# Building the PEER gate matrix in two half-width pieces inside the expert loop, on eight cores

## The reference, cut to what matters

```python
scores = jnp.einsum("thpd,hpkd->thpk", qry, sub_keys)
s_top, i_top = lax.top_k(scores, PEER_TOPK)
cand = s_top[:, :, 0, :, None] + s_top[:, :, 1, None, :]
cand_idx = i_top[:, :, 0, :, None] * 128 + i_top[:, :, 1, None, :]
best, pos = lax.top_k(cand.reshape(n_tok, 8, -1), PEER_TOPK)
idx = jnp.take_along_axis(cand_idx..., pos, axis=-1)
gate = jax.nn.softmax(best, axis=-1)
...
act = gelu(einsum("td,thkd->thk", tb, u_tab[ib]))
out = einsum("thk,thkd->td", gb * act, v_tab[ib])
```

## Time and profile before

| what | us |
|---|---|
| median of 3 executions | 8333.69 (8250.29 to 8431.59) |
| the profiled execution's own time | 8357.25 |
| its slowest core (core 4), first to last instruction | 8355.7 |
| the other cores | 8289.5 to 8339.1 |
| start of the first scatter on core 4 | 4684.88 |

### The profile page before, as it was taken

The page is one execution under the profiler, slowest core; times in us unless marked ns, Lnnn a source line. Parts: engine busy times, 40 slices in busy tenths (PEclk is TensorE's granted clock), DMA queues, the critical chain, the costliest instruction groups (busy, mean ns, idle before and its releaser), DMA issues.

```text
span 8355.7 us, 116273 instructions; the slowest of 8 cores (8289.5 to 8355.7 us)
## 1 busy us (share of the span) xinstructions
PE 5202.0 (62%) x37168; PEld 3963.2 (47%) x37168; DVE 3898.4 (47%) x6582; ACT 2563.6 (31%) x4998; POOL 2637.1 (32%) x2252
## 2 busy tenths in 40 slices
PE   2666666666666666666662185675848485775949
PEld 2555555555555544554551153444535253543635
DVE  3343333344444444444433854547374654547260
ACT  1333333334343333334330122222222222222221
POOL 3222222222222222222210334334353534344353
PEclk7777777778888777777775587786968686777868
DMA  3133334330000000000002054363625254452637
GB/s 66 26 54 54 51 52 57 57 61 11 11 9 16 11 21 21 21 15 17 21 26 56 0 187 152 127 212 101 212 82 197 88 200 136 143 195 101 212 103 238
DMA packets 225330, 714.45 MB, mean 86 GB/s; under 512 B 20704, under 2 KB 70496, under 8 KB 220512
## 3 DMA queue, kind: packets, MB, share of 16 engines
q1 hardware_dynamic: 215520, 625.16, 22.6%
q0 software_dynamic: 9216, 81.86, 7.2%
HBM read 763.62 MB, written 92.27 MB: 102 GB/s over the span
## 4 chain that ended last, share of the span: by engine, by line
PE 42%; DVE 29%; issue 14%; ACT 9%; DMA 2%; POOL 2%; DVEq 1%; ACTq 0%; POOLq 0%; SPq 0%
PE p_bank L202 41%; DVE arena L236 18%; ACT arena L225 5%; ACT L225 3%; POOL arena L236 2%; PE p_bank L207 1%; DVE arena L261 1%; DVE arena L1096 1%; ACT arena L230 1%; DVE arena L1093 1%; DVE arena L247 1%; DVEq L166 1%; DVE arena L1092 1%; DVE arena L1095 1%; DMA arena<-w_in_tm 1%
## 5 line engine op out<-in xcount | busy, mean ns | idle before, releaser
L202 PE MATMUL p_bank<-arena 128*128 128x512 bf16 (+10 forms) x36160 | 5067.6, 305 | 2511.1 <-DVE arena L236 1099.8
L202 PEld LDWEIGHTS p_bank<-arena 128*128 128x128 bf16 (+3 forms) x36160 | 3844.4, 145 | 3720.7 <-issue 3147.5
L236 POOL TENSOR_TENSOR arena<-arena 128x256 bf16<-128x256 bf16 (+3 forms) x2128 | 2529.3, 1195 | 4798.2 <-ACT arena L225 1634.6
L236 DVE TENSOR_TENSOR arena<-arena 128x512 f32<-128x512 f32 (+8 forms) x1984 | 2394.9, 1232 | 1157.0 <-ACT arena L225 889.0
L225 ACT ACTIVATE arena<-p_bank 128x256 bf16<-128x256 f32 (+6 forms) x1648 | 632.7, 384 | 2008.8 <-PE p_bank L202 1921.9
L236 DVE TENSOR_TENSOR arena<-arena,p_bank 128x512 f32<-128x512 f32 (+2 forms) x688 | 420.5, 611 | 1633.5 <-PE p_bank L202 1541.9
L230 ACT COPY arena<-p_bank 128x512 f32<-128x512 f32 (+3 forms) x1120 | 607.3, 547 | 1128.9 <-PE p_bank L202 1010.8
L225 ACT ACT_TABLE_LOAD x341 | 437.5, 1283 | 995.8 <-DVE arena L236 723.9
L230 ACT CAST arena<-p_bank 128x512 bf16<-128x512 f32 x688 | 398.2, 581 | 952.7 <-PE p_bank L202 915.0
L207 PE MATMUL p_bank<-arena 128*128 128x128 f32 (+1 forms) x1008 | 164.1, 312 | 623.2 <-DVE arena L236 539.1
L207 PEld LDWEIGHTS p_bank<-arena 128*128 128x128 f32 (+1 forms) x1008 | 128.4, 157 | 651.9 <-issue 651.7
(11 more groups left out here) (30 smaller groups left out, 668.7 us busy)
## 6 DMA issues: line engine op xcount, KB each, us to landing
arena<-UT_bf SPq DMA_DIRECT2D x512, 512.0 KB, 5.5
arena<-V_bf SPq DMA_DIRECT2D x512, 512.0 KB, 4.4
UT_bf<-UT POOLq DMA_DIRECT2D x16, 2048.0 KB, 24.4
V_bf<-Vt POOLq DMA_DIRECT2D x16, 2048.0 KB, 35.7
arena<-xT SPq DMA_DIRECT2D x48, 528.0 KB, 5.0
arena<-x_scr SPq DMA_DIRECT2D x32, 512.0 KB, 4.7
ob_scr<-arena SPq DMA_DIRECT2D x16, 512.0 KB, 3.1
arena<-ob_scr SPq DMA_DIRECT2D x16, 512.0 KB, 5.9
```

The lines of the kernel that those rows point to most:

```text
L202: self.P.op("pe", lambda e: e.matmul(o, lhsT=l, rhs=r, start=start, stop=stop), reads=_bufs(lhsT, rhs), writes=_bufs(out))
L236: self.P.op(eng, lambda e: e.tensor_tensor(out=o, in0=x, in1=y, op=op), reads=_bufs(a, b), writes=_bufs(out))
```

## The change: what it does

The gate matrix becomes two tiles, `GsH[0]` for columns 0 to 63 and `GsH[1]` for columns 64 to 127. A half is made by 32 steps, each of which makes the full `Ac` (DVE comparison of 1024 elements and POOL product of 1024 elements, as before), half of `Bc` (512 elements), eight matmuls of 64 columns into one bank, the "prep" bank, and one copy of 512 elements, on ACT for even steps and on DVE for odd ones. So `Ac` is made twice for every block.

The steps are called in the expert loop. In its first half (i2 = 0 to 63) the 32 steps for this block's columns 64 to 127 are mixed with the 80 prep steps of the next block, two of these 112 steps after each iteration, until i2 = 55. In its second half the 32 steps for the next block's columns 0 to 63 follow, one after each of i2 = 64 to 95. Ahead of block 0 one half is made on its own. The last block has no prep and no second list; its 32 steps stand after i2 = 0 to 31.

```diff
-    Gs = P.sb("Gs", [128, TB, 128], BF16)
+    GsH = [P.sb("GsA", [128, TB, 64], BF16), P.sb("GsB", [128, TB, 64], BF16)]
...
-    def scatter(pb):
+    def scatter_half_steps(pb, hf):
         aT_ = abwT[pb]; a16_ = abT16[pb]
+        st = []
         for sb_i in range(TB // TS):
-            t0 = sb_i * TS
-            Ac = Acol[sb_i % 2]; Bc = Bcol[sb_i % 2]
-            io_bc = (iot16, iot16.t.unsqueeze(1).to_broadcast([128, TS, 128]))
-            O.tt(V(Ac), io_bc, (a16_, bc_last(a16_.t[:, 0, t0:t0 + TS], 128)), ALU.is_equal)
-            O.tt(V(Ac), V(Ac), (aT_, bc_last(aT_.t[:, 2, t0:t0 + TS], 128)), ALU.mult, eng="pool")
-            O.tt(V(Bc), io_bc, (a16_, bc_last(a16_.t[:, 1, t0:t0 + TS], 128)), ALU.is_equal)
-            for q4 in range(TS // 4):
-                bk = pbank("loop" if (sb_i * (TS // 4) + q4) % 4 else "prep")
-                for q in range(4):
-                    tl = q4 * 4 + q
-                    O.mm((bk, pv4(bk)[:, q, :]), (Ac, Ac.t[:, tl, :]), (Bc, Bc.t[:, tl, :]))
-                O.cp((Gs, Gs.t[:, t0 + q4 * 4:t0 + q4 * 4 + 4, :]), (bk, pv4(bk)), eng="act")
+            def s_sc(sb_i=sb_i):
+                t0 = sb_i * TS
+                ci = sc_ctr[0]; sc_ctr[0] += 1
+                Ac = Acol[ci % 2]; Bc = Bcol[ci % 2]
+                io_bc = (iot16, iot16.t.unsqueeze(1).to_broadcast([128, TS, 128]))
+                io_h = (iot16, iot16.t[:, 64 * hf:64 * hf + 64].unsqueeze(1).to_broadcast([128, TS, 64]))
+                O.tt(V(Ac), io_bc, (a16_, bc_last(a16_.t[:, 0, t0:t0 + TS], 128)), ALU.is_equal)
+                O.tt(V(Ac), V(Ac), (aT_, bc_last(aT_.t[:, 2, t0:t0 + TS], 128)), ALU.mult, eng="pool")
+                O.tt((Bc, Bc.t[:, :, 0:64]), io_h, (a16_, bc_last(a16_.t[:, 1, t0:t0 + TS], 64)), ALU.is_equal)
+                bk = pbank("prep")
+                for tl in range(TS):
+                    O.mm((bk, bk.t[:, tl * 64:(tl + 1) * 64]), (Ac, Ac.t[:, tl, :]), (Bc, Bc.t[:, tl, 0:64]))
+                O.cp((GsH[hf], GsH[hf].t[:, t0:t0 + TS, :]), (bk, bk.t[:, 0:TS * 64].rearrange("p (t i) -> p t i", t=TS)),
+                     eng=("act" if sb_i % 2 == 0 else "dve"))
+            st.append(s_sc)
+        return st
...
-    def expert_loop(pb, side):
+    def expert_loop(pb, side1, side2):
         hT_ = h2T[pb]
-        per = (len(side) + 127) // 128 if side else 0
+        side = side1
+        per = (len(side1) + 59) // 60 if side1 else 0
...
-                O.tt(V(ga), V(ab), (Gs, Gs.t[:, :, i2]), ALU.mult, eng="pool")
+                gh = GsH[i2 // 64]
+                O.tt(V(ga), V(ab), (gh, gh.t[:, :, i2 % 64]), ALU.mult, eng="pool")
...
                 for _ in range(per):
                     if si < len(side):
                         side[si](); si += 1
+                if i2 == 63:
+                    while si < len(side):
+                        side[si](); si += 1
+                    side = side2; si = 0
+                    per = (len(side2) + 59) // 60 if side2 else 0
...
     for blk in range(NB):
         pb = blk % 2
-        scatter(pb)
-        side = prep_steps(blk + 1, 1 - pb) if blk + 1 < NB else []
-        expert_loop(pb, side)
+        pr_ = prep_steps(blk + 1, 1 - pb) if blk + 1 < NB else []
+        sh_ = scatter_half_steps(pb, 1)
+        side1 = []
+        for i in range(max(len(pr_), len(sh_))):
+            if i < len(sh_):
+                side1.append(sh_[i])
+            lo = (i * len(pr_)) // max(1, len(sh_)); hi = ((i + 1) * len(pr_)) // max(1, len(sh_))
+            side1 += pr_[lo:hi] if i < len(sh_) else []
...
+        side2 = scatter_half_steps(1 - pb, 0) if blk + 1 < NB else []
+        expert_loop(pb, side1, side2)
         final(blk)
```

More of the change, by code:

```diff
@@ L1146, in prep_steps @@
         return st
-    def scatter(pb):
+    sc_ctr = [0]
+    def scatter_half_steps(pb, hf):
         aT_ = abwT[pb]; a16_ = abT16[pb]
+        st = []
         for sb_i in range(TB // TS):
-            t0 = sb_i * TS
-            Ac = Acol[sb_i % 2]; Bc = Bcol[sb_i % 2]
-            io_bc = (iot16, iot16.t.unsqueeze(1).to_broadcast([128, TS, 128]))
-            O.tt(V(Ac), io_bc, (a16_, bc_last(a16_.t[:, 0, t0:t0 + TS], 128)), ALU.is_equal)
-            O.tt(V(Ac), V(Ac), (aT_, bc_last(aT_.t[:, 2, t0:t0 + TS], 128)), ALU.mult, eng="pool")
-            O.tt(V(Bc), io_bc, (a16_, bc_last(a16_.t[:, 1, t0:t0 + TS], 128)), ALU.is_equal)
-            for q4 in range(TS // 4):
-                bk = pbank("loop" if (sb_i * (TS // 4) + q4) % 4 else "prep")
-                for q in range(4):
-                    tl = q4 * 4 + q
-                    O.mm((bk, pv4(bk)[:, q, :]), (Ac, Ac.t[:, tl, :]), (Bc, Bc.t[:, tl, :]))
-                O.cp((Gs, Gs.t[:, t0 + q4 * 4:t0 + q4 * 4 + 4, :]), (bk, pv4(bk)), eng="act")
+            def s_sc(sb_i=sb_i):
[14 more added lines that the diff above has]
+        return st
     NG = 128 // IG
@@ L1214, in final @@
                      (obank[tt][dh], obank[tt][dh].t[:, :]), ALU.add)
-            O.act((Gs, Gs.t[:, 0:8, :].rearrange("p a b -> p (a b)")), V(xb), AF.Square, accum=(smf, smf.t[:, tt:tt + 1]))
+            O.act((GsH[1], GsH[1].t[:, 0:16, :].rearrange("p a b -> p (a b)")), V(xb), AF.Square, accum=(smf, smf.t[:, tt:tt + 1]))
             O.act((smf, smf.t[:, tt:tt + 1]), (smf, smf.t[:, tt:tt + 1]), AF.Sqrt, scale=1.0 / 1024, bias=EPS)
@@ L1222, in phase2_build @@
         s_()
+    for s_ in scatter_half_steps(0, 0):
+        s_()
     for blk in range(NB):
         pb = blk % 2
-        scatter(pb)
-        side = prep_steps(blk + 1, 1 - pb) if blk + 1 < NB else []
-        expert_loop(pb, side)
+        pr_ = prep_steps(blk + 1, 1 - pb) if blk + 1 < NB else []
[6 more added lines that the diff above has]
+            side1 += pr_[lo:hi] if i < len(sh_) else []
+        if len(pr_) and len(sh_) == 0:
+            side1 = pr_
+        side2 = scatter_half_steps(1 - pb, 0) if blk + 1 < NB else []
+        expert_loop(pb, side1, side2)
         final(blk)
```

## The result

The changed kernel takes 9918.71 us (median of 10 executions, 9877.92 to 9942.69) where the kernel before, in the same session, takes 8314.54 (8234.48 to 8431.59): a ratio of 1.1964, with a 95% interval of 1.192 to 1.2008. It is 20% slower. The forecast of 9700 was 2.2% low and its range of 9150 to 10150 holds the result.

The account below looks back on a forecast made before the run. Before, DVE bound the scatter and PE the loop; mixed in, a ring of waits binds scatter iterations. 144 + 7 x 640 + 412 = 5036 us against 3671, +1365 on 8357, gives 9722, forecast as 9700; range 9150 to 10150.

Parts of the forecast that it names:

- The ring through PE, ACT, POOL and PE again: Scatter iterations: U, Gelu, GA, product and scatter matmuls wait in a circle, costing their sum, 6.3 us against 1.98 plain.
- The steps are hidden: Rival, chance 0.05: in the loop, scatter matmuls find their product finished; a gain of 612 us, time about 7720.
- it cancels: Rival, chance 0.05: a scatter iteration takes 4.0 us, which would give the time of the kernel before.
- slow throughout: Rival, chance 0.12: PE at 1.2 GHz and the product at 2.74 us; scatter iteration 7.4 us, time 10300.
- the ring alone, fast: Rival, chance 0.16: PE stays at 2.4 GHz and DVE keeps up; scatter iteration 5.2 us, time 8820.
- One sign of being wrong: First half of the loop: the prediction is wrong if PE's waits lie on DVE for much longer than 4 us.
- first half of the loop: Per block, 32 scatter and 80 prep steps over 56 iterations, then 8 plain: 2 x (48 + 122) + 16 = 356 us.
- Two tenths for the odd steps: Scatter iteration: DVE's copy and then its next comparison on odd steps raise 6.1 to 6.3 us.
- The product 2.1: POOL's product in a scatter iteration: 2.1 us, the mean of 1.8 alone and 2.4 behind a half comparison.
- I leave it: Final part of a block: kept at 19 us, since the next block's first scatter step waits on DVE behind the adds.
- DMA: nothing: Loads of the kernel: the same loads over a longer time, so no cost.
- DVE's 255 and POOL's 224 fit under: Loop, if the steps were hidden: DVE's 255 us and POOL's 224 us of work per block fit under its time.

Follow-up runs that it names:

- e1: The changed kernel with each scatter step's eight matmuls and copy called one scatter step later: 8825.84 us, ratio 1.070 to the kernel before.
- e3: The changed kernel with all scatter copies on ACT, none on DVE: 9427.74 us, ratio 1.1392 to the kernel before.
- e11: The changed kernel with both half scatters ahead of the loop, not mixed in, and prep steps one per iteration: 9500.21 us, ratio 1.139.
- e2: The changed kernel with the next block's first table loads issued before this block's final stores: 9954.33 us, ratio 1.206.
- e6: The changed kernel with matmuls and copy one scatter step later and all scatter copies on ACT: 8703.99 us, ratio 1.056.
- e12: The changed kernel with eight idle 512-column matmuls on PE ahead of each scatter step's matmuls in the loop: 9627.42 us, ratio 1.1549.

## Why the prediction was right, and where it was off

**The mechanism is shown.** The ring through PE, ACT, POOL and PE again was forecast from the order of the calls, and e1 removes most of it by that order alone. "The steps are hidden" and "it cancels" are out by the ratio; "slow throughout" by the windows (clock 0.63 and 0.75 in the two parts with scatter, products of 1.85 with DVE idle), "the ring alone, fast" by the same clock. One sign of being wrong was there in part: PE's waits for DVE in the first half, 78.6 us in 12 waits up to 8.9, are longer than the 4 us named. The forecast did count DVE's side in that half, and the half came out 14 us over.

**Direction and size of each term.** By the loop ends of core 5 (5495.3, 6159.7, 6822.8, 7487.0, 8152.3, 8820.8, 9482.8) a block is 664.6 us in the mean, where 640 was forecast. In the fourth block:

| term | forecast | measured |
|---|---|---|
| half ahead of block 0 | 144 | 138.4 |
| boundary | 19 | 23.5 |
| first half of the loop | 356 | 369.7 |
| 32 scatter iterations | 202 (6.3 each) | 212 (6.63 each) |
| 32 plain iterations | 63 | 59 |
| last block | 412 | 409.4 |

Seven blocks are 172 us over, and phase 2 begins at 4711.6 on this core where it began at 4684.9 on core 4 before. Together 199; less 6 for the half ahead and 3 for the last block, it makes the 190 by which the span of 9912 exceeds 9722. Phase 1 is untouched, and I take those 27 us as spread between cores and executions: in the kernel before, POOL's first product starts between 4674 and 4791 on its eight cores.

**Where a step of it was off.**

- *"Two tenths for the odd steps".* e3 shows 0.9, and a ring of 5.75, not 6.1, without them: two errors that all but cancelled, and that is luck. What I had missed is the order that DVE's copy imposes. It keeps DVE waiting for PE and then sends two steps' comparisons through in one burst, just when POOL has its GA and product, so that this pair takes 4.15 and not 2.67. The same 0.9 is in e11, whose half steps take 281 / 64 = 4.39 where 1.13 + 0.6 + 1.8 is 3.53; there I had priced it (1.9 for a pair, in the half ahead of block 0), in the ring not.
- *"The product 2.1".* The mean is 67.8 / 32 = 2.12, and 1.85 alone, as forecast, but for another reason: I had put 2.4 where a half comparison is ahead, and in e3, where the comparisons are over before POOL begins (7590.61 + 1.83 is 7592.44), the mean is 1.90. It is the bursts that make 2.12 of it. And GA was taken unchanged at 0.82, which it is not:

```profile
L236 POOL TENSOR_TENSOR arena<-arena 128x1024 bf16<-128x1024 bf16 x32 | 67.8, 2120 | 0.0
L236 POOL TENSOR_TENSOR arena<-arena 128x256 bf16<-128x256 bf16 x32 | 39.0, 1220 | 105.7 <-ACT arena L225 104.8 <-PE p_bank L202 1.0
```

  GA's mean is 1.22 (1220 ns, busy 39.0 us in 32). GA too seems to wait for a running comparison. GA and product together are 3.34 where the forecast had 0.82 + 0.1 + 2.1 = 3.02, and these 0.32 are what 6.63 has over 6.3. The comparisons grow as well: the half ones, put at 0.6, show 1.03 in the mean in this window.
- *"I leave it" for the final part, "DMA: nothing".* The boundary is 4.5 us longer. The UT loads of the next block are issued by SP right behind the final part's store, at 6841.65. Before, the scatter of 129 us stood between these loads and the first U; now the first U waits for them:

```profile
6841.16 0.34 SPq L276 DMA_DIRECT2D out<-arena  x1
6841.65 0.32 SPq L276 DMA_DIRECT2D arena<-UT_bf  x1
6846.27 1.87 PE L202 MATMUL p_bank<-arena 128*128 128x256 bf16 x8 [22.98 <-DMA arena<-UT_bf]
```

  e2 shows that loading earlier gains nothing here, since the Gelu stands behind the same final part.
- *The first half.* 14 us over. PE's waits for DVE are the 78.6 us above; how they divide between the top-k steps and the copies was not taken apart.

**The second bound.** Even with the ring opened, the change does not pay, and that part of the argument was only half in the prediction. It had "DVE's 255 and POOL's 224 fit under" the loop, as if they could run side by side, although the paragraph on the product had just shown that they take turns. In e6 both are without a gap at 4.06 us per step. The Trainium skill (SBUF — State Buffer, Who interferes with whom) says that a DVE instruction with two SBUF inputs and a GpSimd instruction that reads SBUF exclude each other; e6 agrees in the main, with 4.06 where the sum of all four is 4.40 and the fuller engine alone would be 2.67. With that 4.06 the hidden case was never open: 64 steps of it are 260 us, the 125 of prep on DVE come on top, and 40 plain iterations are 79, with the boundary 484, where e6's block takes about 495 and the old one 466. Doubling the `Ac` work is what an overlap could not win back.

The Trainium skill (Perfetto Trace Analysis, Optimization Strategy) says that interleaving regimes bound by different engines may improve performance; the prediction had named it for the chance of a gain, at 0.05. Here the interleaved kernel is 20% slower, of which the order of the calls accounts for 13 points (1.1964 against 8825.84 / 8245.91 = 1.070 in e1).

**Open.** What makes 4.06 out of 4.40, and which pairs do overlap, was not settled. The gains of e3 and e1 do not add up: behind e1's order the copies on ACT bring 0.014 (1.070 to 1.056 in e6) where alone they bring 0.057. How much of each gain is the clock was not separated. Nor was a version without the doubled `Ac`, with a later consumer and a gap ahead of the gate, run.

## What to carry to other kernels

When work is mixed into a loop on engines that execute in order, write down for one iteration who stands behind whom in each queue and who waits for whom: if the path closes, the iteration costs the sum of the path and not the busiest engine, and calling the consumer one step later than its producer opens it. Before counting on overlap, check in the trace whether the two engines progress together at all; a duration that grows from 1.2 to 2.9 us beside another engine's instruction says that they don't. And a small operation, such as a copy, on an engine that is idle is not free if it waits for the slow side of the ring, because all that stands behind it comes in a burst.

## What I had not expected of the hardware

- GA, 256 elements on POOL, shows 0.82 us in the plain loop and 1.22 in the mean beside DVE's comparisons: a row's duration seems to hold the wait for the other engine, for short instructions too.
- PE busy for 55% of a stage had a granted clock of 0.63, for 79% of 0.78 (e12), and eight idle matmuls in each scatter step of the loop made the kernel 3.5% faster.
- Small instructions are dear for their size: tensor_scalar on 128x128 bf16 takes 0.41 us on DVE with POOL idle (3.27 for eight), an activation with a scale 0.47 on ACT (1.88 for four), where one comparison of 1024 elements takes 1.13.
